# Two of the four weight sums of each seven-product group made by DMAs instead of by VectorE

## The reference, cut to what matters

```python
def first_block(x, ...):
    a = rms_norm(h, norm_mix[i])
    h = h + stick_breaking_mixer(a, sb_w_qkv[j], sb_w_o[j])
    h = h + sq_relu_mlp(rms_norm(h, norm_mlp[i]), mlp_w1[i], mlp_w2[i])   # relu(h @ w1)**2 @ w2
    return rms_norm(h, final_norm)

def second_block(x, ...):
    z = rms_norm_2(x, pre_mix_g[l]) @ w_in[l]       # attention and pooling on z, then
    m = jnp.concatenate([a, p], axis=-1) @ w_o[l]
    x = x + rms_norm_2(m, post_mix_g[l])
    up = causal_dwconv(rms_norm_2(x, pre_ffn_g[l]) @ w_up[l], conv_w[l], conv_b[l])
    y = (gelu(up[..., :D_FF_2]) * up[..., D_FF_2:]) @ w_down[l]
    return x + rms_norm_2(y, post_ffn_g[l])
```

## Time and profile before

| what | value |
|---|---|
| median of 3 runs | 2083.42 us (2083.16 to 2085.51) |
| profiled execution, its own time | 2083.09 us |
| its span, first to last instruction | 2081.4 us |
| mean granted TensorE clock | 0.999 of full speed |
| PE, DVE, ACT, POOL busy | 2069.7, 1387.0, 1126.7, 59.9 us |
| HBM read, written | 432.75 MB, 35.13 MB |

### The profile page before, as it was taken

How to read it: one execution, slowest core, us unless ns; L and a number is a source line. 1 busy time by engine, 2 the same in 40 slices (tenths; PEclk the granted TensorE clock), 3 DMA queues, 4 the chain that set the end, 5 groups by cost and what they waited for, 6 DMA issues and landing times.

```text
span 2081.4 us, 24042 instructions
## 1 busy us (share of the span) xinstructions
PE 2069.7 (99%) x9232; PEld 1713.9 (82%) x9232; DVE 1387.0 (67%) x1574; ACT 1126.7 (54%) x1369; POOL 59.9 (3%) x55
## 2 busy tenths in 40 slices
PE   9999999999999999999999999999999999999998
PEld 8888888888888888888888888888888888888877
DVE  6546555665884669666876655566766885576795
ACT  7555554555554555455655544455555554555563
POOL 3000000000000000000002000000000000000010
PEclk9999999999999999999999999999999999999999
DMA  8687656787657775777677787667787666777853
GB/s 297 197 255 232 190 187 218 253 235 254 219 188 222 231 245 201 226 222 245 222 254 239 219 249 228 199 207 222 245 249 239 203 213 212 238 226 246 259 192 142
DMA packets 291907, 469.50 MB, mean 226 GB/s; under 512 B 18512, under 2 KB 82128, under 8 KB 291280
## 3 DMA queue, kind: packets, MB, share of 16 engines
q1 hardware_dynamic: 290928, 463.46, 70.8%
q10 hardware_dynamic: 864, 4.49, 0.7%
HBM read 432.75 MB, written 35.13 MB: 225 GB/s over the span
## 4 chain that ended last, share of the span: by engine, by line
PE 96%; DVE 2%; ACT 1%; issue 0%; DMA 0%; ACTq 0%; DVEq 0%
PE ps L1752 96%; DVE Wl L1356 1%; ACT Wh L1132 0%; DVE E L1615 0%; DVE T L1459 0%; PE ps L1755 0%; ACT E L1276 0%; DMA gains<-in_gains_dram 0%; ACT T L1192 0%; DVE hid L1524 0%; ACT hid L1235 0%; DVE wsum L1367 0%; DVE E L1621 0%; DVE wsum L1362 0%; ACT L1110 0%
## 5 line engine op out<-in xcount | busy, mean ns | idle before, releaser
L1356 DVE TENSOR_TENSOR Wl<-raw,Wh 128x1024 fp32r<-128x1024 f32 x743 | 909.1, 1243 | 568.7 <-ACT Wh L1132 562.0
L1752 PE MATMUL ps<-Wh,aHL 128*128 128x512 f32 x3712 | 1148.7, 390 | 0.7 <-ACT aHL L1160 0.4
L1132 ACT ACTIVATE Wh<-raw 128x1024 fp32r<-128x1024 f32 x743 | 770.5, 1056 | 538.8 <-PE ps L1752 505.3
L1752 PEld LDWEIGHTS ps<-Wh,aHL 128*128 128x128 f32 x3712 | 696.7, 188 | 146.4 <-issue 1.7
L1752 PE MATMUL ps<-Wl,aHL 128*128 128x512 f32 x1856 | 722.1, 389 | 0.0
L1752 PE MATMUL ps<-Wh,hid 128*128 128x512 f32 x1488 | 464.8, 390 | 3.1 <-DVE Wl L1356 2.3
L1752 PEld LDWEIGHTS ps<-Wl,aHL 128*128 128x128 f32 x1856 | 348.4, 188 | 71.6
L1752 PEld LDWEIGHTS ps<-Wh,hid 128*128 128x128 f32 x1488 | 279.3, 188 | 64.4 <-DVE Wl L1356 3.3
L1752 PE MATMUL ps<-Wl,hid 128*128 128x512 f32 x744 | 289.5, 389 | 0.0
L1752 PEld LDWEIGHTS ps<-Wl,hid 128*128 128x128 f32 x744 | 139.7, 188 | 28.9
L1752 PE MATMUL ps<-Wh,oHL 128*128 128x512 f32 x512 | 159.0, 390 | 0.0
(11 more groups left out here) (202 smaller groups left out, 921.3 us busy)
## 6 DMA issues: line engine op xcount, KB each, us to landing
raw<-in_mlp_w_dram SPq DMA_DIRECT2D x256, 512.0 KB, 4.8
raw<-in_w_up_dram SPq DMA_DIRECT2D x176, 512.0 KB, 4.6
raw<-in_sb_w_qkv_dram SPq DMA_DIRECT2D x93, 512.0 KB, 5.4
raw<-in_w_down_dram SPq DMA_DIRECT2D x88, 512.0 KB, 5.0
raw<-in_w_in_dram SPq DMA_DIRECT2D x64, 512.0 KB, 5.3
passed_strip<-T SPq DMA_DIRECT2D x104, 256.0 KB, 3.6
T<-passed_strip SPq DMA_DIRECT2D x208, 128.0 KB, 4.6
raw<-in_sb_w_o_dram SPq DMA_DIRECT2D x32, 512.0 KB, 5.1
```

Source lines behind the costliest of these rows:

```text
L1132: e.activation(Wh[:, i % NW, c], src, ACT.Copy).then_inc(st["hi"][0], 1)
L1356: e.tensor_tensor(Wl[:, i % NW, c], src, Wh[:, i % NW, c].bitcast(F32), ALU.subtract).then_inc(st["lo"][0], 1)
L1752: return e.matmul(o, l, r, start=start, stop=stop, skip_group_check=True)
```

## The change

The tile `wsum` grows from three strips to four. Sum 0 goes into strip 0 in groups with an even number `m` within their pair and into strip 2 in the others; the running sum is always strip 1, between the two, and the last sum strip 3. A new step `add_loads` stands ahead of `weight_sums` and runs on GpSimd alone. It issues three DMAs of 128 x 512 float32, 256 KB each, and two of them add onto what their destination holds (`accum_op`):

1. W11 from HBM into the sum tile, once `free["sums"]` and this tile's own last use are over;
2. W22 from HBM added onto W12 in the raw slot `b`, once `b` has landed;
3. W12 from HBM added onto the sum tile, once the first has landed.

DVE's `weight_sums` keeps two additions, the running sum and the last sum. It waits for the third DMA as well. The rounding of `s1` waits for the second. What `free["sums"]` held after a group is now held apart: `free["sum0"]` and `free["sum2"]` (the low half of `s2` is made) and `free["grouped"]` (that of `s3`), and `fold` and `mix_tokens` wait for it. `free["sums"]` itself keeps the last mark of a fold or of `mix_tokens`. In PE's `s2` the two terms change places where sum 0 lies in strip 2.

```diff
--- before.py
+++ after.py
@@ -59,7 +59,7 @@
 def plan_program(sem):
     p = Plan(sem)
     step, done, after, later = p.step, p.done, p.after, p.later
-    free = {n: [] for n in ("QK1", "T0", "T1", "E", "zs", "set0", "set1", "set2", "mT", "qk0", "qk1", "v0", "v1", "A0", "A1", "sums")}
+    free = {n: [] for n in ("QK1", "T0", "T1", "E", "zs", "set0", "set1", "set2", "mT", "qk0", "qk1", "v0", "v1", "A0", "A1", "sums", "sum0", "sum2", "grouped")}
     st = {}
     now = [0]
 
@@ -158,7 +158,7 @@
 
         d = [done("token_mixed") for c in range(4)]
         hi, lo = done("mixed_hi"), done("mixed_lo")
-        step("mix_tokens", mov=mov, src=src, k=k, n=n, need=[*need, *free["sums"]], d=d, hi=hi)
+        step("mix_tokens", mov=mov, src=src, k=k, n=n, need=[*need, *free["sums"], *free["grouped"]], d=d, hi=hi)
         free["sums"] = [lo]
         later(1, lambda: step("mix_low", mov=mov, k=k, n=n, hi=hi, lo=lo))
         for j in range(k, k + n):
@@ -170,7 +170,7 @@
         def f(sets, k):
             copied = done("fold_copied")
             marks = [done("folded") for i in range(5 if fresh else 8)]
-            step("fold", to=to, s4=s4, k=k, sums_free=list(free["sums"]), copied=copied, marks=marks, fresh=fresh)
+            step("fold", to=to, s4=s4, k=k, sums_free=[*free["sums"], *free["grouped"]], copied=copied, marks=marks, fresh=fresh)
 
             def second():
                 step("fold_rest", to=to, s4=s4, marks=marks, fresh=fresh)
@@ -774,12 +774,18 @@
 
         q, n = p.pieces[i], int(p.pieces[i]["kind"][1])
         if n == 0:
-            made = {m: done("weights_added") for m in (1, 3, 2, 4)}
-            step("weight_sums", a=raw_of[i] % NRAW, b=raw_of[i + 1] % NRAW, need=[landed(i), landed(i + 1), *free["sums"]], made=made)
-            free["sums"] = [(lo_sem, i + 4)]
-            for m in (1, 2, 3):
-                p.pieces[i + m]["made"] = made[(3, 2, 4)[m - 1]]
-        step("split", i=i, part=q["kind"], slot=raw_of.get(i, 0) % NRAW, loaded=landed(i) if n == 0 else q["made"],
+            at = 2 * (q["m"] % 2)
+            first, added, right = done(f"first_landed{at}", 16), done(f"second_added{at}", 16), done(f"right_added{at}", 16)
+            step("add_loads", i=i, at=at, b=raw_of[i + 1] % NRAW, b_landed=landed(i + 1), need=[*free["sums"], *free[f"sum{at}"]],
+                 first=first, added=added, right=right)
+            made = [done("weights_added") for m in range(2)]
+            step("weight_sums", at=at, a=raw_of[i] % NRAW, b=raw_of[i + 1] % NRAW,
+                 need=[added, landed(i), landed(i + 1), *free["sums"], *free["grouped"]], made=made)
+            free[f"sum{at}"], free["grouped"] = [(lo_sem, i + 3)], [(lo_sem, i + 4)]
+            for m, token in zip((1, 2, 3), (right, *made)):
+                p.pieces[i + m]["made"] = token
+                p.pieces[i + m]["sum_at"] = at
+        step("split", i=i, part=q["kind"], at=q.get("sum_at"), slot=raw_of.get(i, 0) % NRAW, loaded=landed(i) if n == 0 else q["made"],
              used=(mm_sem, i - NW + 1), hi=(hi_sem, i + 1), lo=(lo_sem, i + 1))
         if i in raw_of:
             load(raw_of[i] + NRAW)
@@ -941,7 +947,7 @@
         mixed_row, = area(("mixed_row", [128, 2048], F32))
         hid2, hidMix2 = area(("hid2", [128, 24, 2 * TOK], F32R), ("hidMix2", [128, 3, 4, TOK], F32R))
         sb("back", [128, 24 * 2 * TOK + 3 * 4 * TOK])
-        wsum = sb("wsum", [128, 3, STRIP])
+        wsum = sb("wsum", [128, 4, STRIP])
         halves = wsum[:, :, :].rearrange("p j n -> p (j n)")
         xn = QK[:, :].rearrange("p (t n) -> p t n", t=2)
         qk = QK[:, :].rearrange("p (g w h q) -> p g w h q", g=2, w=2, h=4)
@@ -1006,9 +1012,10 @@
 
         def to_split(st):
             if st["part"] == "s2":
-                return halves[:, 0:2 * STRIP], slice(0, 2 * STRIP)
+                at = st["at"] // 2
+                return halves[:, at * STRIP:(at + 2) * STRIP], slice(0, 2 * STRIP)
             if st["part"] == "s3":
-                return halves[:, 2 * STRIP:3 * STRIP], slice(0, STRIP)
+                return halves[:, 3 * STRIP:4 * STRIP], slice(0, STRIP)
             return rawv[:, st["slot"], :], slice(0, 2 * STRIP)
 
         def mixed_rows(st):
@@ -1359,12 +1366,9 @@
                     made = st["made"]
                     for t in st["need"]:
                         e.wait_ge(*t)
-                    e.tensor_tensor(wsum[:, 0, :], a[:, 0, :], b[:, 0, :], ALU.add).then_inc(made[1][0], 1)
-                    e.tensor_tensor(b[:, 0, :], b[:, 0, :], b[:, 1, :], ALU.add).then_inc(made[3][0], 1)
-                    e.wait_ge(*made[1])
-                    e.tensor_tensor(wsum[:, 1, :], wsum[:, 0, :], b[:, 1, :], ALU.add).then_inc(made[2][0], 1)
-                    e.wait_ge(*made[2])
-                    e.tensor_tensor(wsum[:, 2, :], wsum[:, 1, :], a[:, 1, :], ALU.add).then_inc(made[4][0], 1)
+                    e.tensor_tensor(wsum[:, 1, :], wsum[:, st["at"], :], b[:, 1, :], ALU.add).then_inc(made[0][0], 1)
+                    e.wait_ge(*made[0])
+                    e.tensor_tensor(wsum[:, 3, :], wsum[:, 1, :], a[:, 1, :], ALU.add).then_inc(made[1][0], 1)
                 elif k == "mix_tokens":
                     d, hi, lo = mixed_rows(st)
                     src = (T1[:, :, :] if st["src"] == "T1" else E4).rearrange("p (k t) q -> p t k q", t=2)
@@ -1686,9 +1690,21 @@
                     e.affine_select(out=v, in_=v, compare_op=ALU.is_gt, fill=0.0, base=0, pattern=[[0, 4], [1, 128]],
                                     channel_multiplier=-1).then_inc(done[0], 1)
 
+            def block(i, t):
+                return source(pieces[i])[:, t, :]
+
             for st in p.steps:
                 k = st["kind"]
-                if k == "consts":
+                if k == "add_loads":
+                    for t in st["need"]:
+                        e.wait_ge(*t)
+                    i, total = st["i"], wsum[:, st["at"], :]
+                    e.dma_start(total, block(i, 0)).then_inc(st["first"][0], 16)
+                    e.wait_ge(*st["b_landed"])
+                    e.dma_start(rawv[:, st["b"], 0:STRIP], block(i + 1, 1), accum_op=ALU.add).then_inc(st["right"][0], 16)
+                    e.wait_ge(*st["first"])
+                    e.dma_start(total, block(i + 1, 0), accum_op=ALU.add).then_inc(st["added"][0], 16)
+                elif k == "consts":
                     e.memset(ident[:, :], 0.0).then_inc(st["set"][0][0], 1)
                     e.memset(tri[:, :], 1.0).then_inc(st["set"][1][0], 1)
                     e.memset(ones[:, :], 1.0).then_inc(st["set"][2][0], 1)
@@ -1777,6 +1793,8 @@
                          "s1": (("d1", side[:, 2, :], q["opens"], True), ("d3", b[:, 0, :], q["opens"], False)),
                          "s2": (("d0", side[:, 1, :], q["opens"], True), ("d2", side[:, 3, :], q["opens"], True)),
                          "s3": (("a22", a[:, 1, :], False, False),)}[q["kind"]]
+                if q["kind"] == "s2" and q["sum_at"]:
+                    terms = terms[::-1]
                 for t, (name, P, starts, ends) in enumerate(terms):
                     c = slice(t * 512, (t + 1) * 512)
                     x, h, l = halves_of[name]
```

## The result

The kernel after took 2139.55 us (median of 4 runs, 2137.32 to 2145.31); beside it the kernel before took 2083.46 (4 runs, 2083.16 to 2085.51). The ratio is 1.0274, with an interval of 1.0261 to 1.0286: 56 us slower. The prediction had the sign right and the size wrong: 7 us slower, range up to 2103.

The account below looks back on a forecast made before the run. TensorE, 99% busy, was taken as the bound, so DVE's relief returns only where PE waits. Terms -1.2 + 4.8 + 1.7 + 1.7 = +7.0 us on the median 2083.42 gave 2090.4 us, range 2082.5 to 2103.

Parts of the forecast that it names:

- The relief of DVE: Two sums fewer per group shorten DVE's run, removing both PE waits for Wl at group 18: gain 1.2 us.
- Group 10: Sum tile free only at the fold's end, then two DMAs in a row, landing at 808.0: PE loses 4.8 us.
- Groups 7 and 13: Late last DMA delays DVE's split to hid (L1524), with 7.4 us from B's landing: PE loses 1.7 us each.
- X = 6.4: Time from landing of load B to landing of the group's last DMA: two 1.0 us issues plus 4.4 us landing.
- accumulating is slow: Rival, chance 0.10: accumulating takes twice 4.4 us; groups 10, 7 and 13 lose 9.2, 6.1 and 6.1; 2104 us or above.
- The other groups: All remaining groups: splits mostly run ahead of PE, so the DMAs' lateness costs nothing there.
- Traffic at nothing: Extra 19 MB on 463 MB, 4% or about 7% with old contents, through queues 71% busy: nothing charged.
- DVE holding up GpSimd: Rival, chance 0.04: GpSimd writes descriptors only once DVE stands still, every group late; some +26 us, 2109.

Follow-up runs that it names:

- The run with groups 4, 10 and 19 put right: Kernel after, but groups 4, 10 and 19, which follow a fold, keep all four sums on VectorE: 2121.88 us, ratio 1.0185.
- with little late: Kernel after with the sum's DMAs ahead of the wait for B, groups 4, 10, 19 on VectorE, third sum tile, tiles moved 2048 bytes: 2084.43 us, ratio 1.0005.

## Why the prediction was wrong

- **The relief of DVE**, -1.2 us at group 18 only: right in place, -1.7 measured. In the kernel after the late DMAs ate it: PE waits 1.81 and 0.93 us at groups 17 and 18.
- **Group 10**, a loss of 4.8 us by a chain of two DMAs of 8.4: right in mechanism; the chain took 9.3 us and PE lost 5.98. The issues were 0.6 and 0.9 us, and the landings after issue 4.1 and 3.4: together within 1 us of my sum, with the parts off both ways.
- **Groups 7 and 13**, 1.7 each by X = 7.4: right in mechanism, too small. X was 8.6 and 8.4, the waits 3.45 and 3.07 us, where before they were 0.37.
- **X = 6.4, the step that failed first.** I built an accumulating landing of 4.4 from one DMA by itself, and added the second only as an issue. By itself that is near (4.2 in quiet). But two are issued together while loads run, and then the second lands 7.9 to 8.3 us after the first one's issue; in the kernel X had a median of 8.7. The rival "accumulating is slow" had its size (8.8 for one landing) and only 0.10 of the chance.
- **"The other groups" at nothing, the step that weighed most:** 27.1 of the 39.6 us of PE's waits for DVE. I argued from ACT's 402 waits that splits run ahead, and did not ask how late the sums may start. The trace of before could have told: there load B landed 2.5 to 9.3 us before the group's first sum, and outside groups 18 and 24 the low halves `Wl` of its pieces were ready 1.8 to 6.6 us before the first matmul that reads them. An X above these two together, and the 1.2 that DVE is shorter, costs PE time. In group 16 the three are 3.15, 1.85 and 1.2, so 6.2 us; X was 8.9, and PE waited 2.58. In group 22 they are 3.8, 1.9 and 1.2, so 6.9; X was 8.4, and PE waited 1.62.
- **Each group taken for itself.** While DVE stands at its first sum for up to 9.6 us no raw slot comes free, so the next loads go out later. B of group 6 shows it, the answer of before in the first fence and of after in the second: 9.7 us later, when PE's own new waits so far came to 4.4 us, so B came 5.3 us later for PE. Group 6 alone had 10.8 us of room (5.5, 4.2 and 1.2) for an X of 10.4; with the 5.3 it was late, by 3.51 us of PE's time. X counts from the landing of B, so a late group can make the next one's B late. The run with groups 4, 10 and 19 put right shows the same at groups 6, 20 and 21, which were no longer late, and not at group 12.

```profile
L1078 SPq DMA_DIRECT2D raw<-in_mlp_w_dram x1: 368/368/368, 592.0 to 592.0; - x1
```

```profile
L1085 SPq DMA_DIRECT2D raw<-in_mlp_w_dram x1: 368/368/368, 601.7 to 601.7; - x1
```

- **The clock, which no term had.** Seven of the waits had 3.4 or 6.8 us at half clock around their end, some 14 of the 54 us. The trace of before has no wait of PE above 1.3 us between its first and last microseconds, so no row bore on it.
- **Traffic at nothing**: right. The same DMAs in another order cost 47 us less, and with little late 1 us in all. DVE holding up GpSimd was not seen: its issues take 0.5 to 0.9 us, 1.2 for one right behind another, and the same with DVE idle (0.54 to 0.9, and 1.2).

A matmul's 0.39 us, which the prediction takes from the earlier trace rows, is in the trace of before, but not in that row.

What stays open: why the last DMA of a group took 9.2 us in group 6 and 4.3 in group 10. In the runs without computation an accumulating DMA took 4.2 alone and at most 7.9 as the second of two beside loads. So 9.2 lies above all that those runs gave, and none sets the loads of group 6 beside it exactly.

## What to carry to other kernels

Before a sum is moved from an engine to a DMA, read for each place when its input lands and when the sum starts, and add the lead of what is built from it: the new path must fit into that, at the load and with the partners it will run beside. An in-order queue that waits for a late DMA delays the loads behind it, so one late group can make the next one late. Order the DMA that somebody waits for ahead of a wait for something else: that alone brought back 47 of 56 us. When tiles are moved to make room, measure the move by itself: 2048 bytes did no harm here, 64 and 2112 bytes cost 19 and 21 us.

## What the runs showed of the hardware

- An accumulating DMA of 256 KB landed 4.1 to 4.2 us after its issue in quiet, a plain one after 3.0; beside two streams of loads 5.4 to 5.9 and 3.0 to 4.7; the second of two accumulating ones 7.3 to 7.7.
- The granted clock of PE fell from 1.0 to 0.50 in or right behind every wait of 3.6 us or more put in, and at none of 1.92 or less. In the kernel after it did so at a wait of 1.85 us (group 21), and in the kernel with 64 bytes less at one of 1.94, and not at those of 2.23 (group 3) and 2.58 (group 16) in after, so the length of the wait alone does not decide.
- A move of the tiles behind `spare` by 64 bytes made the matmuls with 512 columns take 391 to 393 ns for 389 to 390, and the kernel 19 us slower; a move by 2112 did the same (2 to 3 ns, 21 us), and one by 2048 left them as they were. Which of the moved tiles matters was not tested.
